# Gate products in pairs in the first attention, and reordered ScalarE and VectorE work around the second mixer

## What is computed

```python
def first_block(x, ...):
    h = h + 0.5 * swiglu(rmsnorm(h, ffn1_norm[l]), ffn1_w_gu[l], ffn1_w_down[l])
    u = rmsnorm(h, mix_norm[l])
    qa, ka, va, qb, kb, vb, qi, ki, wi, g = jnp.split(u @ w_in[l], SPLIT_POINTS, axis=-1)
    ...
    out_a = dsa_attention(qa, ka, va, qi, ki, wi, bias_dsa)
    out_b = moba_attention(qb, kb, vb, bias_moba)
    gates = jax.nn.sigmoid((g + b_gate[l]).astype(jnp.float32)).astype(h.dtype)
    g_a, g_b = jnp.split(gates, 2, axis=-1)
    mixed = g_a * (out_a @ w_branch_dsa[l]) + g_b * (out_b @ w_branch_moba[l])
    h = h + mixed @ w_out[l]
    h = h + 0.5 * swiglu(rmsnorm(h, ffn2_norm[l]), ffn2_w_gu[l], ffn2_w_down[l])

def mla_mixer(h, cos, sin, w_dkv, g_q, g_kv, w_uq, w_ukv, w_o):
    lat = h @ w_dkv
    c_q = rmsnorm_2(lat[..., :MLA_Q_LORA], g_q)
    c_kv = rmsnorm_2(lat[..., MLA_Q_LORA:MLA_Q_LORA + MLA_KV_LORA], g_kv)
    k_pe = lat[..., MLA_Q_LORA + MLA_KV_LORA:][:, :, None, :]
    q = (c_q @ w_uq).reshape(B, S, MLA_HEADS, MLA_NOPE + MLA_ROPE)
    kv = (c_kv @ w_ukv).reshape(B, S, MLA_HEADS, MLA_NOPE + MLA_V)
    ...
    o = blocked_causal_softmax_attn(q, k, v, (MLA_NOPE + MLA_ROPE) ** -0.5)
    return o.reshape(B, S, MLA_HEADS * MLA_V) @ w_o
```

## Time and profile before

| | us |
|---|---|
| median of 3 runs | 1268.73 (1268.25 to 1268.86) |
| the profiled execution | 1268.47 |
| its span | 1266.7 |
| PE busy | 1255.2 (99%) |
| DVE busy | 763.9 (60%) |
| ACT busy | 652.2 (51%) |
| POOL busy | 16.9 (1%) |

### The profile page before, as it was taken

The page is one execution under the profiler, slowest core; times in us unless marked ns, Lnnn a source line. Parts: engine busy times, 40 slices in busy tenths (PEclk is TensorE's granted clock), DMA queues, the critical chain, the costliest instruction groups (busy, mean ns, idle before and its releaser), DMA issues.

```text
span 1266.7 us, 17026 instructions
## 1 busy us (share of the span) xinstructions
PE 1255.2 (99%) x6856; PEld 1086.8 (86%) x6856; DVE 763.9 (60%) x1084; ACT 652.2 (51%) x844; POOL 16.9 (1%) x21
## 2 busy tenths in 40 slices
PE   9999999999999999999999999999999999999998
PEld 7888888888888888888888899989888888999896
DVE  6545448788675554447865675454563656754554
ACT  6454437464455444436853564443465755643433
POOL 0000000001000000000000000000000000000001
PEclk9999999999999999999999999999999999999999
DMA  8755545554533755545633265554565332665540
GB/s 295 291 182 192 192 151 206 218 181 139 178 133 124 247 179 196 179 134 171 235 131 117 84 241 194 197 179 133 189 232 180 120 104 96 227 218 176 195 133 34
DMA packets 39487, 221.74 MB, mean 175 GB/s; under 512 B 4502, under 2 KB 5670, under 8 KB 23921
## 3 DMA queue, kind: packets, MB, share of 16 engines
q1 hardware_dynamic: 36800, 213.94, 49.3%
q0 software_dynamic: 1024, 4.22, 1.0%
q10 hardware_dynamic: 1584, 2.48, 0.7%
HBM read 219.56 MB, written 1.07 MB: 174 GB/s over the span
## 4 chain that ended last, share of the span: by engine, by line
PE 96%; ACT 2%; DVE 1%; issue 0%; ACTq 0%; DVEq 0%
PE ps L429 23%; PE ps L431 23%; PE ps L430 23%; PE ps L672 5%; PE ps L671 5%; PE ps L670 5%; PE ps L1723 2%; PE ps L1745 2%; PE ps L463 1%; PE ps L1732 1%; PE ps L708 1%; PE ps L1113 1%; ACT whi L371 1%; PE ps L2452 1%; PE ps L2454 1%; PE ps L2453 1%
## 5 line engine op out<-in xcount | busy, mean ns | idle before, releaser
L379 DVE TENSOR_TENSOR wlo<-w_raw,whi 128x2048 fp32r<-128x2048 f32 (+3 forms) x238 | 458.6, 1933 | 373.2 <-ACT whi L371 373.0
L371 ACT ACTIVATE whi<-w_raw 128x2048 fp32r<-128x2048 f32 (+4 forms) x242 | 391.0, 1623 | 406.2 <-PE ps L431 300.1
L429 PE MATMUL ps<-whi,xt_h 128*128 128x512 f32 (+3 forms) x740 | 291.0, 393 | 0.6 <-DVE wlo L403 0.2
L431 PE MATMUL ps<-whi,xt_l 128*128 128x512 f32 (+3 forms) x740 | 285.3, 386 | 0.0
L430 PE MATMUL ps<-wlo,xt_h 128*128 128x512 f32 (+3 forms) x740 | 284.6, 385 | 0.0
L429 PE MATMUL ps<-whi,ot_h 128*128 128x512 f32 x570 | 225.4, 395 | 1.1 <-ACT v L1466 0.7
L431 PE MATMUL ps<-whi,ot_l 128*128 128x512 f32 x570 | 222.3, 390 | 0.0
L430 PE MATMUL ps<-wlo,ot_h 128*128 128x512 f32 x570 | 222.1, 390 | 0.0
L429 PEld LDWEIGHTS ps<-whi,xt_h 128*128 128x128 f32 x740 | 139.0, 188 | 29.6 <-issue 3.6
L431 PEld LDWEIGHTS ps<-whi,xt_l 128*128 128x128 f32 x740 | 138.9, 188 | 27.8
L430 PEld LDWEIGHTS ps<-wlo,xt_h 128*128 128x128 f32 x740 | 139.1, 188 | 25.8
(11 more groups left out here) (264 smaller groups left out, 1054.6 us busy)
## 6 DMA issues: line engine op xcount, KB each, us to landing
w_raw<-ffn_mid SPq DMA_DIRECT2D x80, 768.0 KB, 4.3
w_raw<-mlp_mid SPq DMA_DIRECT2D x56, 1024.0 KB, 5.0
w_raw<-w_qkv SPq DMA_DIRECT2D x12, 1024.0 KB, 5.1
w_raw<-w_sb_qkv SPq DMA_DIRECT2D x12, 1024.0 KB, 5.1
w_raw<-w_xkv SPq DMA_DIRECT2D x8, 1024.0 KB, 5.0
w_raw<-ffn_first SPq DMA_DIRECT2D x8, 512.0 KB, 4.1
w_raw<-w_gate_b SPq DMA_DIRECT2D x4, 1024.0 KB, 5.1
w_raw<-w_gate_a SPq DMA_DIRECT2D x4, 1024.0 KB, 5.1
```

The lines of the kernel that those rows point to most:

```text
L371: nc.scalar.activation(whi[:, s, 0:tiles * width], w_raw[:, s, 0:tiles * width], ACT.Copy).then_inc(w_hi, 1)
L379: nc.vector.tensor_tensor(wlo[:, s, 0:tiles * width], w_raw[:, s, 0:tiles * width], whi[:, s, 0:tiles * width].bitcast(F32), ALU.subtract) ...
L429: nc.tensor.matmul(acc, hi, whi[:, s, c], start=start, stop=False)
L431: return nc.tensor.matmul(acc, lo, whi[:, s, c], start=False, stop=stop)
```

## The change

There are five edits, and none adds or removes a matmul or a load.

1. `Ffn.vector`, for the network ahead of the second mixer: the second half of the residual is updated before the second part of a split, not after it.
2. `Project.latents_scalar` and `LatentUp.scalar`: ScalarE's split `next_hi` of the last latent chunk moves behind the copies of the latent rows (`take_rows`, `root_k`); each later split moves behind the copy that followed it; `take_v` copies one row tile at a time, with `take_turned` between the two.
3. The split of `v[1]` + 4 leaves `LatentUp` and becomes `late` in `Attend`: ScalarE does it behind group 0's exponentials, VectorE behind group 0's scaling.
4. PE takes the gate blocks by `gate_pairs`: blocks 1 and 2 in iteration 0, 3 and 4 in iteration 2, and so on to 13 and 14 in iteration 12 and 15 in iteration 14.
5. ScalarE and VectorE keep `gate_products`, so their own order in the first attention is as before.

```diff
@@ Ffn.vector
-                    part_lo(dve, chunks[0] + RING, 2, 1)
-                    residual_vector(dve, self.down_full, self.scale, 1)
+                    if self.following == "mla":
+                        residual_vector(dve, self.down_full, self.scale, 1)
+                        part_lo(dve, chunks[0] + RING, 2, 1)
+                    else:
+                        part_lo(dve, chunks[0] + RING, 2, 1)
+                        residual_vector(dve, self.down_full, self.scale, 1)
@@ Project.latents_scalar
                 next_hi(act, second.n[0][0])
-                next_hi(act, second.n[1][0])
@@ LatentUp.scalar
             def scalar(self, act):
+                before = self.before
                 self.take_rows(act, 0)
                 self.take_rows(act, 1)
                 self.root_k(act)
+                next_hi(act, before.units[-1].n[1][0])
+                self.take_q(act, 0)
+                before.take(act, before.units[-1])
+                self.take_q(act, 1)
                 next_hi(act, self.pe)
-                self.take_q(act, 0)
-                self.before.take(act, self.before.units[-1])
-                self.take_q(act, 1)
+                self.take_q(act, 2)
                 next_hi(act, self.q[0])
-                self.take_q(act, 2)
+                self.take_q(act, 3)
                 next_hi(act, self.q[1])
-                self.take_q(act, 3)
                 self.take_k(act, 0)
                 self.take_k(act, 1)
                 self.aside.scalar(act)
-                next_hi(act, self.k[0])
                 self.take_k(act, 2)
                 self.take_k(act, 3)
+                next_hi(act, self.k[0])
+                self.take_v(act, 0, 0)
                 self.take_turned(act)
+                self.take_v(act, 0, 1)
                 next_hi(act, self.k[1])
-                self.take_v(act, 0)
+                self.take_v(act, 1, 0)
+                self.take_v(act, 1, 1)
                 next_hi(act, self.v[0])
-                self.take_v(act, 1)
-                next_hi(act, self.v[1])
@@ LatentUp.vector
                 next_lo(dve, self.v[0])
-                next_lo(dve, self.v[1])
@@ Attend.tensor
                     if self.select:
-                        for i in gate_products(g):
+                        for i in gate_pairs(g):
                             self.gates[i // 4].tensor(pe, i % 4)
@@ Attend.scalar
+                    if self.late is not None and g == 0:
+                        next_hi(act, self.late)
                     for filler, step in fill_steps(self.fillers, g):
@@ Attend.vector
                     if self.turned and g < len(self.groups):
                         self.scale_vector(dve, g)
+                    if self.late is not None and g == 0:
+                        next_lo(dve, self.late)
@@
+        def gate_pairs(g):
+
+            return [i for i in range(1, 16) if (i - 1) // 2 * 2 == g]
@@
+        mla_attend.late = mla_up.v[1]
```

More of the change, by code:

```diff
@@ L1461, in take_k, with take_v @@
                                      ACT.Copy).then_inc(self.evac, 1)
[L1463 to L1467, removed]
+            def take_v(self, act, block, t):
+                act.wait_ge(self.full, 11 + NT * block + t)
+                nc.scalar.activation(v[:, t, block * TW:(block + 1) * TW], bankA[t],
+                                     ACT.Copy).then_inc(self.evac, 1)
             def root_k(self, act):
@@ L1694, in __init__ @@
                 self.fillers, self.bank_free = fillers, bank_free or {}
+                self.late = None
                 self.groups, self.need, self.select = groups, need, select
```

## The result

The changed kernel takes 1271.03 us (median of 20 runs, 1270.52 to 1271.72), the kernel before on the same chips 1268.47 (20 runs, 1267.87 to 1269.25). The ratio is 1.0020, with an interval from 1.0014 to 1.0026: 2.56 us slower, at the very edge of what can be told from no change. The profiled execution took 1271.0, its span is 1269.2 (before: 1268.47 and 1266.7).

A forecast was written before the change was run, and what follows sets the result against it. TensorE is busy 99% of the span, so only its waits count. 1268.47 less 2.1 won in the second mixer plus 4.2 lost in the first attention is 1270.6; own range 1269.4 to 1271.6, wider range 1268.6 to 1272.4.

The forecast's parts named there:

- rival (B): First attention: VectorE late at every second block that opens a bank, two more waits of some 0.5: 1272.1; chance 0.26.
- The wait of iteration 2: First attention, second block of the pair: PE waits 1.7 us for VectorE to read the bank.
- Iterations 3, 7 and 9: First attention: PE waits 0.55 at each turn of finished rows, 1.65 together, with no block in between.
- Iteration 13: First attention, last rows: PE waits 1.15 where a block of 2.86 stood.
- The restarts: First attention: longer products behind each of five waits, 0.1 each, counted only in the bound of 5.5 lost.
- No wait at 6 and 10: First attention, second blocks of these iterations: VectorE needs 2.5 to 3.2 against 3.6 for PE, so no wait.
- The saving of the pairs: First attention, entry into a run of products: between 0 and 1.3 for seven merged pairs, 0.3 taken.
- Rival (C): Both attentions: pairing wins 1.3, finished-row waits hidden, no wait of 0.65: 1267.3, or 1266.1 with iteration 13's hidden; chance 0.08.
- The orders around the second mixer: Second mixer: five waits of PE go, 2.97 gross, less 0.25 given back at the rotated keys' transposes: 2.72.
- Not late for anything that PE asks for: Ffn's tail: the split now behind the residual comes in time while PE is busy with its transposes (1.09).
- The knot: Second attention, turn of group 1: new wait of 0.65 behind VectorE's half of the moved split, leaving 2.1 won.
- rival (E): First attention: PE falls to 1.2 GHz after the wait of 1.7, one iteration's 4.96 doubles: 1275.5; chance 0.03.

The follow-up runs named there:

- the run with the late residual: Orders and moved split only (1266.19), with the residual's second half behind the split of 0.95 again: 1267.05 us.
- two experiments: Kernel before with pairs in odd iterations: 1282.0; fastest kernel with the low half of the turned input ahead of the split of 1.75: 1268.04.
- both forecasts made in this way: Kernel before with all pairs, block 2's gate read one iteration earlier on VectorE: 1272.32; kernel before with pairs only in iterations 0, 4 and 10: 1269.85.
- two of three further moves in the second mixer: Orders and moved split, VectorE's half behind group 1: 1266.06; on that, filler's split one iteration later: 1266.64, or low half ahead of split of 1.75: 1268.04.
- one kernel: Orders and moved split, VectorE's half behind group 1, plus the low half of the turned input ahead of the split of 1.75: 1268.04.
- another's: Second mixer's orders alone on the kernel before, with the split of v[1] + 4 back ahead of the second attention: 1267.87.

## Why the prediction was right, and where not

The forecast was 1270.6, with 1269.4 to 1271.6 as its own range, and 1271.03 came: against the profiled execution 2.5 lost instead of 2.1. The verdict that was called likeliest, within 0.2% on the slow side, is met only at its edge: 0.20%, with an interval that reaches to both sides of it. Both sums were too small, by 0.7 lost and by 0.2 won, which partly cancelled: the places of the waits in the first attention were foreseen, but that the total came within 0.4 is in part luck. The largest term that both sums lack is the slower products behind each wait. The prediction had it in its bounds and in rival (B), at 0.1 for a restart, and at nothing in the sum.

*The wait of iteration 2*, 1.7: the wait itself is 1.69, and 1.85 with the slower products behind it. VectorE reads the gate at 293.81, where the prediction had it begin at 293.78. The reason given ("VectorE loses here the 2.7 in which it now has nothing to do") was the right one, but the prediction used it for this wait alone. The backlog stays until VectorE has a pause, at 299.13: with the wait removed, the loss came back in iteration 3 to all but 0.97, and with the bank opening left in place 1.3 to 1.4 was still lost.

*Iterations 3, 7 and 9*, three times 0.55: from the start of the last matmul of the values to that of the turn 0.71, 0.81 and 0.81 pass, where 0.11 is normal, so 0.60, 0.70 and 0.70, together 2.0 for 1.65. *Iteration 13*, 1.15: 1.12 by the windows, which is a wait of 1.2 and 0.06 for the restart, less 0.15 that the pair of iteration 12 saves. *The restarts*, at nothing in the sum: 0.16 in iteration 2, 0.05 at each of the next three waits and these 0.06, together 0.37. *No wait at 6 and 10*: right; those runs take 5.66 and 5.74.

*The saving of the pairs*, 0.3 for all seven, was about right. With waits and restarts taken off, the pairs of iterations 0, 2, 4, 6, 8, 10 and 12 save 0.01, 0.03, 0.07, 0.08, 0.03, 0.04 and 0.15, together 0.4. Where a score stands in the iteration that is left without products, a pair gives back most of what it wins: the turn starts 0.22 behind the last score matmul, where a product started 0.03 behind it. The last pair has no score behind it and keeps the whole 0.15: its 24 products take 5.56, two runs of 12 took 2.86 each. Rival (C), with 0.18 to a pair, is refuted: two pairs alone, in iterations 4 and 10, save 0.14, and the waits that it had as hidden are there. The terms add up to 1.7, 2.0, 1.2 and 0.4 less 0.4, and 4.90 was measured. The bound of 5.5 for what the attention loses held. The Trainium skill's rule (TensorE: Matmul & The Clock Gate, Back-to-back issue gap), by which the pairs win nothing and the sum was 0.3 higher, is not borne out by these 0.4.

*The orders around the second mixer*, 2.72 net: at 579.53 the kernel after is 4.90 late, at its first scores 1.84 (634.36 against 632.52), so 3.06 were won. Mis-sized were the waits, 3.5 and not 2.97, since the first products behind each of the five were slow as well, by some 0.1: the 36 products of the values take 8.29 instead of 9.34, so 1.05 went where 0.86 was counted. Of this 0.40 was given back and not 0.25: 0.15 at the transposes of the rotated keys and 0.25 at a place that the prediction did not have. "Not late for anything that PE asks for" was wrong: behind the later split the low half of the turned input comes late, and PE loses that 0.25 at the second weight chunk. That cost next to nothing in the end, by the run with the late residual. The residual's edit alone is worth 0.7 to 0.9 us.

*The knot*, the new wait of 0.65 at the turn of group 1: it is 0.57. Its cause is shown: with VectorE's half of the split behind group 1 it is gone. Another 0.15 is lost at the turn of group 0 (6.52 behind the first scores instead of 6.37), which the prediction did not look at. This loss is there in all runs with the moved split, 0.19 with VectorE's half behind group 1, and its cause is open. That the split pays for its place was not in the prediction as a number: 1.6 of the 2.3 hang on it.

*The clock*, rival (E): at waits of 1.5 the granted clock stays at 1.00, and the 20 executions of the kernel after lie within 1.2 us. What the slower clock costs is shown by two experiments, and the change doesn't pay it. Rival (B)'s time, 1272.1, was not reached; its restarts were real, its additional waits absent.

## What to carry to other kernels

Work that is taken from one stretch of PE's queue and given to the one before is paid by the engine that works an iteration behind PE: it idles through the double block and then has its full backlog with half the cover. Count that engine's queue from the end of its idle time to its next pause, rather than each wait by itself; both forecasts made in this way (1272.4 and 1269.9) hit the time to 0.1 us, one of them its loss to 0.2. And give each wait 0.05 to 0.16 more for the slow products behind it: here ten waits made 0.9 us of that. And before a split or copy is moved "behind", name who reads it and what it would now stand behind: two of three further moves in the second mixer failed on that.

## What was unexpected about the hardware

After an idle of 3.4 us and one of 2.5 us on PE the granted clock fell to the 1.2 GHz level, 1.5 and 0.8 us after work had resumed and for 3.4 us each time. An idle of 1.8 (start to start 2.15) was followed by such a stretch in the profiled execution of one kernel, and by none after 2.25 in another's; both kernels' times lie in two groups about 1.5 apart, the lower one the larger. That this is the clock is shown for the upper group of one kernel; no execution of the lower group of that kernel was profiled, and in the other kernel it was only the lower. The mean granted clocks of all eleven executions lean the same way: 0.9980 in the upper group against 0.9991 in the lower for the first kernel, 0.9975 against 0.9987 for the other, where 3.4 us at half clock make 0.0013 of the whole. The Trainium skill (TensorE: Matmul & The Clock Gate, What's actually happening) has the clock set by how busy PE has just been, and the traces agree in that every such stretch between 7 and 1260 us stands behind an idle of PE. Here an idle near 2 us was a lottery with a stake of about 1.5 us, while 20 executions with 1.5 us of idle showed nothing.
